# Statistics of the second LayerNorm moved to ScalarE for token tiles 0 to 2, both affine passes on VectorE

## What is computed

```python
def _layernorm(x, g, b, eps=1e-5):
    mu = jnp.mean(xf, axis=-1, keepdims=True)
    var = jnp.mean(jnp.square(xf - mu), axis=-1, keepdims=True)
    y = (xf - mu) * lax.rsqrt(var + eps) * g + b

x = _layernorm(DN_ALPHA * x + mix @ w_out[l], ln1_g[l], ln1_b[l])
gate, up = jnp.split(x @ w_gate_up[l], 2, axis=-1)
x = _layernorm(DN_ALPHA * x + (jax.nn.silu(gate) * up) @ w_down[l], ln2_g[l], ln2_b[l])
```

## Time and profile before

| what | value |
|---|---|
| median of 3 runs | 2053.0 us (2051.79 to 2054.34) |
| profiled execution | 2054.76 us, its span 2053.0 us |
| granted TensorE clock over the span, mean | 0.997 |
| busy share of the span: PE, DVE, ACT, POOL | 99%, 64%, 32%, 18% |
| tail: DVE's first tail add to the last instruction of the span | 2001.47 to 2053.0 us |

### The profile page before, as it was taken

The page is one execution under the profiler, slowest core; times in us unless marked ns, Lnnn a source line. Parts: engine busy times, 40 slices in busy tenths (PEclk is TensorE's granted clock), DMA queues, the critical chain, the costliest instruction groups (busy, mean ns, idle before and its releaser), DMA issues.

```text
span 2053.0 us, 32475 instructions
## 1 busy us (share of the span) xinstructions
PE 2028.1 (99%) x12569; PEld 1798.4 (88%) x12569; DVE 1316.7 (64%) x1899; ACT 654.4 (32%) x1034; POOL 369.1 (18%) x177
## 2 busy tenths in 40 slices
PE   8999999999999999999999999999999999999997
PEld 6777888766888999998989999898998989999895
DVE  3079993463114786776857667585776857677688
ACT  3011000454000263342524334243442524334250
POOL 2555556144566400000000000000000000000001
PEclk9999999999999999999999999999999999999999
DMA  7333444400524323342333424234242434424242
GB/s 206 102 83 82 102 102 103 128 22 21 208 100 123 80 81 120 87 127 83 84 123 85 142 66 139 80 109 124 83 134 73 113 93 115 122 85 124 86 149 82
DMA packets 292057, 214.05 MB, mean 104 GB/s; under 512 B 9526, under 2 KB 256118, under 8 KB 290010
## 3 DMA queue, kind: packets, MB, share of 16 engines
q1 hardware_dynamic: 291850, 211.97, 35.5%
q10 hardware_dynamic: 80, 0.13, 0.0%
HBM read 207.76 MB, written 4.19 MB: 103 GB/s over the span
## 4 chain that ended last, share of the span: by engine, by line
PE 97%; DVE 2%; issue 0%; DMA 0%; ACT 0%; SPq 0%; DVEq 0%
PE psum L1102 13%; PE psum L1100 13%; PE psum L1098 13%; PE psum L1139 7%; PE psum L1140 7%; PE psum L1141 7%; PE psum L728 7%; PE psum L729 7%; PE psum L730 7%; PE psum L960 3%; PE psum L962 3%; PE psum L961 3%; PE psum L940 1%; PE psum L878 1%; PE psum L869 1%; PE psum L852 1%
## 5 line engine op out<-in xcount | busy, mean ns | idle before, releaser
L1098 PE MATMUL psum<-act,w_room 128*128 128x256 f32 x1344 | 374.7, 279 | 0.0
L1100 PE MATMUL psum<-act,w_room 128*128 128x256 f32 x1344 | 374.7, 279 | 0.0
L1102 PE MATMUL psum<-act,w_room 128*128 128x256 f32 x1344 | 374.7, 279 | 0.0
L1861 DVE TENSOR_TENSOR w_room<-raw,w_room 128x1024 fp32r<-128x1024 f32 x210 | 256.7, 1223 | 128.0 <-ACT w_room L1381 128.0
L1861 DVE TENSOR_TENSOR w_room<-raw_c,w_room 128x1024 fp32r<-128x1024 f32 x164 | 200.8, 1224 | 174.2 <-ACT w_room L1381 174.2
L1381 ACT CAST w_room<-raw 128x1024 fp32r<-128x1024 f32 x212 | 223.4, 1054 | 224.8 <-PE psum L1141 133.0
L1139 PE MATMUL psum<-w_room,h 128*128 128x512 f32 x672 | 261.9, 390 | 0.0
L1140 PE MATMUL psum<-w_room,h 128*128 128x512 f32 x672 | 261.6, 389 | 0.0
L1141 PE MATMUL psum<-w_room,h 128*128 128x512 f32 x672 | 261.5, 389 | 0.0
L1100 PEld LDWEIGHTS psum<-act,w_room 128*128 128x128 f32 x1344 | 252.7, 188 | 0.4
L1098 PEld LDWEIGHTS psum<-act,w_room 128*128 128x128 f32 x1344 | 252.7, 188 | 0.4
(11 more groups left out here) (238 smaller groups left out, 3592.1 us busy)
## 6 DMA issues: line engine op xcount, KB each, us to landing
raw_c<-in_w_gate_up SPq DMA_DIRECT2D x84, 512.0 KB, 4.1
raw<-in_w_gate_up SPq DMA_DIRECT2D x84, 512.0 KB, 5.0
raw_c<-in_w_down SPq DMA_DIRECT2D x82, 512.0 KB, 3.8
raw<-in_w_in SPq DMA_DIRECT2D x30, 1024.0 KB, 5.9
raw<-in_w_out SPq DMA_DIRECT2D x16, 1024.0 KB, 5.2
proj<-in_x_t SPq DMA_DIRECT2D x4, 1024.0 KB, 10.6
acc<-in_x SPq DMA_DIRECT2D x1, 4096.0 KB, 12.5
raw<-in_w_gate_up SPq DMA_DIRECT2D x4, 1024.0 KB, 5.8
```

The source lines that it names most:

```text
L1098: nc.tensor.matmul(out_ap, stat_hi[:, cols], mov_hi[:, k, :], start=opens and k == 0, stop=False, skip_group_check=not opens)
L1100: nc.tensor.matmul(out_ap, stat_hi[:, cols], mov_lo[:, k, :], start=False, stop=False, skip_group_check=not opens)
L1102: mm = nc.tensor.matmul(out_ap, stat_lo[:, cols], mov_hi[:, k, :], start=False, stop=k == kh - 1, skip_group_check=not opens)
L1861: nc.vector.tensor_tensor(lo, src, hi.bitcast(F32), ALU.subtract).then_inc(lo_ready, 1)
```

## The change

ScalarE computes the statistics of tiles 0, 1 and 2. For each column block it copies the block into a part of `act` that is no longer read, with the sum as the accumulator's output; a copy of the four sums, scaled by -1/2048, gives minus the mean; a Square over 2048 columns with that as its bias gives the sum of squares; a square root gives the deviation. VectorE no longer runs `bn_stats` and the joining of parts for these tiles. It runs both affine passes for all tiles: (acc + minus_mean) * gain, then acc * rstd + bias, without the small shift instruction. The passes of tile `i - 1` stand after step 1 of tile `i` (steps 5, 9 and 13), no longer after the tile's own last step. Tile 3 keeps `bn_stats` and its four pieces. GpSimd's two passes and ScalarE's scaling of tile 0 are gone, and the wait for gain and bias stands after `late_piece(3)`, no longer ahead of step 3. Three small SBUF tiles (96 bytes a partition) are put ahead of `stats`, so that everything laid out behind them moves by 96 bytes.

```diff
         raw = sb("raw", [P, 2, SLAB])
+        tail_sums = sb("tail_sums", [P, TT, 4])
+        minus_mean = sb("minus_mean", [P, TT])
+        square_sum = sb("square_sum", [P, TT])
         stats = sb("stats", [P, TT, 4, 6])
...
-            pool.wait_ge(ln_loaded, 64)
-            pool.wait_ge(normal_done, 1)
-            nc.gpsimd.tensor_tensor(acc[:, 0, :], acc[:, 0, :], ln2_gain[:, :], ALU.mult).then_inc(gained, 1)
-            pool.wait_ge(gained, 1)
-            nc.gpsimd.tensor_tensor(acc[:, 0, :], acc[:, 0, :], ln2_bias[:, :], ALU.add).then_inc(y_ready[0], 1)
...
             after_high(3, FF_CHUNKS - 1)
-            for i in range(TT):
-                deviation(i, 1)
-                if i == 0:
-                    act.wait_ge(rstd_ready, TT + i + 1)
-                    nc.scalar.activation(acc[:, i, :], acc[:, i, :], ACT.Identity, bias=shift[:, i:i + 1],
-                                         scale=rstd[:, i:i + 1]).then_inc(normal_done, 1)
+            act.wait_ge(gran_done, c43.q + 7)
+            added = 16 * last + TILES0 + 16
+            for i in range(TT - 1):
+                for n in range(4):
+                    act.wait_ge(tile_added, added + 4 * i + n + 1)
+                    nc.scalar.activation(act_hi[:, n, :], acc[:, i, n * SEQ:(n + 1) * SEQ], ACT.Copy,
+                                         accum_out=tail_sums[:, i, n:n + 1]).then_inc(part_summed, 1)
+                act.wait_ge(part_summed, 4 * i + 4)
+                nc.scalar.activation(act_lo[:, 0, 0:4], tail_sums[:, i, :], ACT.Copy, scale=-1.0 / D_MODEL,
+                                     accum_out=minus_mean[:, i:i + 1]).then_inc(mean_known, 1)
+                act.wait_ge(mean_known, i + 1)
+                nc.scalar.activation(act_hi[:, 0:4, :].rearrange("p k s -> p (k s)"), acc[:, i, :], ACT.Square,
+                                     bias=minus_mean[:, i:i + 1], accum_out=square_sum[:, i:i + 1])\
+                    .then_inc(squares_summed, 1)
+                act.wait_ge(squares_summed, i + 1)
+                nc.scalar.activation(std[:, i:i + 1], square_sum[:, i:i + 1], ACT.Sqrt, bias=eps[:, :],
+                                     scale=1.0 / D_MODEL).then_inc(std_done, 1)
+            act.wait_ge(var_ready, TT + 1)
+            nc.scalar.activation(std[:, TT - 1:TT], moments[:, TT - 1, 1:2], ACT.Sqrt, bias=eps[:, :])\
+                .then_inc(std_done, 1)
...
+            def affine(i):
+                y = acc[:, i, :]
+                ve.wait_ge(std_done, TT + i + 1)
+                link(nc.vector.reciprocal(rstd[:, i:i + 1], std[:, i:i + 1]))
+                link(nc.vector.scalar_tensor_tensor(out=y, in0=y, scalar=minus_mean[:, i:i + 1], in1=ln2_gain[:, :],
+                                                    op0=ALU.add, op1=ALU.mult))
+                nc.vector.scalar_tensor_tensor(out=y, in0=y, scalar=rstd[:, i:i + 1], in1=ln2_bias[:, :],
+                                               op0=ALU.mult, op1=ALU.add).then_inc(y_ready[i], 1)
+
             for e in range(16):
                 i, n = e // 4, e % 4
-                if e == 3:
-                    ve.wait_ge(ln_loaded, 64)
-                add_tail(i, n, e % 8, e + 1, added + e + 1)
+                add_tail(i, n, e % 8, e + 1, added + e + 1, with_stats=i == TT - 1)
                 if e == 0:
                     late_piece(2)
                     late_piece(3)
-                if n == 3:
-                    moments_of(i)
...
-                        scale_and_shift(i, cols, TT + i + 1, y_ready, 1)
+                    ve.wait_ge(ln_loaded, 64)
+                if i > 0 and n == 1:
+                    affine(i - 1)
+            moments_of(TT - 1)
+            for n in range(4):
+                cols = slice(n * SEQ, (n + 1) * SEQ)
+                centre(TT - 1, cols, TT + 1, 1)
+                if n == 0:
+                    ve.wait_ge(std_done, 2 * TT)
+                    link(nc.vector.reciprocal(rstd[:, TT - 1:TT], std[:, TT - 1:TT]))
+                y = acc[:, TT - 1, cols]
+                nc.vector.scalar_tensor_tensor(out=y, in0=y, scalar=rstd[:, TT - 1:TT], in1=ln2_bias[:, cols],
+                                               op0=ALU.mult, op1=ALU.add).then_inc(y_ready[TT - 1], 1)
```

More of the change, by code:

```diff
@@ L353, in build @@
         late_low = sem("late_low")
-        normal_done = sem("normal_done")
-        gained = sem("gained")
+        part_summed = sem("part_summed")
+        mean_known = sem("mean_known")
+        squares_summed = sem("squares_summed")
         p1_copied = sem("p1_copied")
@@ L1781, in add_down, with add_tail @@
                 nc.vector.tensor_tensor(cols, cols, psum[:, i, :], ALU.add).then_inc(tile_added, 1)
-            def add_tail(i, n, bank, tiles, count):
+            def add_tail(i, n, bank, tiles, count, with_stats):
                 cols = acc[:, i, n * SEQ:(n + 1) * SEQ]
@@ L1786, in add_tail @@
                 nc.vector.tensor_tensor(cols, cols, psum[:, bank, :], ALU.add).then_inc(tile_added, 1)
-                ve.wait_ge(tile_added, count)
-                link(nc.vector.bn_stats(stats[:, i, n, :], cols))
+                if with_stats:
+                    ve.wait_ge(tile_added, count)
+                    link(nc.vector.bn_stats(stats[:, i, n, :], cols))
             def moments_of(i):
```

## The result

The changed kernel takes 2071.54 us (median of 6 runs, 2068.32 to 2072.06), the kernel before 2052.69 (6 runs, 2051.79 to 2054.34): 18.9 us more by the medians. The forecast was 2052.0 us, with 2049.4 to 2055.0 as its range. The profiled execution has a span of 2069.9 us at a granted clock of 0.997, as before, so it isn't the clock.

The account below looks back on a forecast made before the run. PE was taken to bound nearly all of the span and DVE's queue the end. Tile 3's joining 0.86 us earlier plus 0.19 for the shift gave 1.05, so 2053.0 - 1.0 = 2052.0 us, range 2049.4 to 2055.0.

Parts of the forecast that it names:

- What bounds the kernel, and what leaves DVE: PE is 97% of the chain, DVE's queue sets the end; the change rids DVE of 7.2 us net.
- rival 4: Moved addresses of acc, x_room and h change the time by 4 us either way; chance 0.05, both signs alike.
- What PE gains: In the tail, step 3's wait for late_piece(2) shrinks, so all later steps of PE come 0.76 us earlier.
- What ScalarE needs: From a tile's last add to its deviation: 4.1 us taken, 3.6 the lower sum, 5.4 for tile 0 with table load.
- The schedule and its sum, 1.05 us: On DVE in the tail, tile 3's joining starts 0.86 us earlier and its dropped shift saves 0.19.
- The rule against the change: Skill page puts adds and multiplies on VectorE; per tile ScalarE spends 5.8 us on what costs DVE 3.4.
- The rivals 1 to 3: PE's wait stays, 2052.7 us, chance 0.12; tile 2's statistics late, 2054.6, 0.08; ScalarE slows tile 2's passes, 2055.7, 0.05.
- The list of what would prove it wrong: DVE waiting for ScalarE ahead of tile 2's passes, a pass above 2.4 us, or moved rows before 2001.

## Why the prediction was wrong

- **What bounds the kernel, and what leaves DVE:** right about the engines, PE over nearly all of the span, DVE at the end. Wrong in the half-sentence "the change touches none of that": the three tiles moved operands of PE's matmuls, which is rival 4 below. The passes take 2.35 us each with POOL silent, and DVE waits for PE ahead of steps 5, 8, 9, 12 and 13.
- **What PE gains:** right. With the tiles last, PE's last matmul of step 13 starts 31.77 us after the first add, 32.64 before: 0.87 earlier, where 0.76 was forecast; no row of PE in the tail waits for a late piece any more, in the changed kernel neither.
- **What ScalarE needs:** right, at the low end. Its timeline in the changed kernel, tile 0 and the end of tile 2:

```profile
2024.72 0.63 ACT L1508 ACTIVATE act<-acc 128x512 fp32r<-128x512 f32 x1 [0.89 <-DVE acc L1798]
2025.26 0.19 ACT L1508 ACTIVATION_READ_ACCUMULATOR act<-acc 128x1 f32 x1
2025.48 0.20 ACT L1511 ACTIVATE act<-tail_sums 128x4 fp32r<-128x4 f32 x1
2025.59 0.19 ACT L1511 ACTIVATION_READ_ACCUMULATOR act<-tail_sums 128x1 f32 x1
2025.81 2.01 ACT L1514 ACTIVATE act<-acc,minus_mean 128x2048 fp32r<-128x2048 f32 x1
2027.72 0.18 ACT L1514 ACTIVATION_READ_ACCUMULATOR act<-acc,minus_mean 128x1 f32 x1
2027.92 1.28 ACT L1518 ACT_TABLE_LOAD   x1
2029.22 0.29 ACT L1518 ACTIVATE std<-square_sum,eps 128x1 f32<-128x1 f32 x1
...
2050.64 0.29 ACT L1518 ACTIVATE std<-square_sum,eps 128x1 f32<-128x1 f32 x1
```

  Tile 0's last add ends at 2024.69 and its deviation is there at 2029.51: 4.8 us, 5.4 forecast. For tile 2 it is 2047.37 to 2050.93: 3.6, the lower bound; 4.1 was taken. One table load, behind tile 0's Square, none after it. Between the read's end at 2027.90 and the load are 0.02 us, and as many between the load's end and the square root, so the drain that the Trainium skill adds to a switch (ScalarE: Activation LUTs, What ACT_TABLE_LOAD costs) is not seen here either.
- **The schedule and its sum, 1.05 us:** right as a term. With the addresses as before the trace shows 1.13. In the changed kernel the tail gained 0.54 only: its own 96 matmuls of w_room with h take 5.6 ns more each, 0.54 us.
- **The rule against the change:** the prediction says that the rows agree, per element, that adds and multiplies belong on VectorE. They don't: a Copy of 512 columns takes 0.63 us on ScalarE and an add or `bn_stats` 0.69 on VectorE. What makes ScalarE dearer here is that it goes over the data twice. Nothing in the forecast hangs on it.
- **The rivals 1 to 3** did not occur: no wait on line 1891's successor, no wait of DVE for ScalarE's deviations, no pass above 2.35.
- **Rival 4, the addresses: here the prediction failed,** in its chance and its price. It had 0.05, both signs alike, and 4 us for its effect; the measured loss in the loop is 17.4 us. The ground was that line 1141 takes 0.39 us with w_room and with x_room as the other operand (the moving one, not the weights as the prediction calls it). Those rows could not speak: in the kernel before, w_room, h and x_room all lie at 192 modulo 256, so the two cases compared had the same distance of 0. They showed that the pace was the same at one distance, not that it doesn't depend on it; and with two decimals a duration would hardly show it, since the slow ones of the changed kernel read 0.39 and 0.40. The kernel's text gave a hint: `SHIFT` sets operands that PE reads together 32 bytes apart by hand, and three small tiles ahead of h change such distances. The move was 128 bytes and not 96, but the prediction drew nothing from its size. The 4 us were 0.2% of the loop, the limit of what a measurement tells, not a bound on the mechanism: 3024 matmuls at 2.0 ns and 2016 at 5.6 give 17 us.
- **The list of what would prove it wrong** named the right row: "if the rows of the stretch before 2001 moved". They moved by 17.44 us.

A page that spoke for ignoring the addresses: the Trainium skill (SBUF — State Buffer, Who interferes with whom) has PE with two independent read ports and says that PE never waits on anyone. Where h alone moved by 128 bytes against w_room, the w_room,h matmuls follow each other by 232.4 ns and not by 226.8. Whether that is to be called waiting no row shows; the measurement decides that the addresses have a price.

## What to carry to other kernels

Put new small tiles behind the big ones, or check that the distances between the tiles that PE reads together (weights and moving operand, modulo 256 bytes here) stay as they were; where PE is 99% busy, as here, 2 to 6 ns a matmul (17 us) outweighed what the change did in the tail (1 us). When a change looks small and the time moves a lot, find the first instruction that is late: if it stands ahead of the edited code, compare the same matmuls by form and from start to start. A row that shows no sensitivity proves something only if the two cases differ in the thing in question.

## What the runs showed of the hardware

- The pace of these fp32 matmuls depends on the distance between the addresses of weights and moving operand within a partition: 113.4 to 119.9 ns for 256 columns, 226.8 to 233.3 ns for 512, over the distances tried, all multiples of 32 bytes. Moving everything alike by 128 left the paces as they were, and so did moving one operand by 256. Why the distance counts no run shows.
- The best distance of those tried differs: 64 bytes for the 256-column matmuls with x_room (tried: 0, 32, 64, 96, 160, 224), 0 for the 512-column ones with h (tried: 0, 32, 64, 128, 192, 224). The same 64 with act moved as well gave 117.8, so a further condition exists that these runs don't name.
- A mean can hide such an effect: with act and w_room unmoved, the single steps of act's matmuls are 116 or 117 ns in the kernel before and 113 to 122 in the changed one, with the same mean of 116.7.
- A group's mean duration shows the direction and not the price: in the changed kernel it rose by 2.5 ns for x_room's matmuls and 5.2 for w_room,h, while the starts came 2.0 and 5.6 later. With act at 64 bytes too, x_room's rose by 3.2 and its starts came 4.4 later.
